# Two layer norms moved into the blocks that use them, x turned in the experts' block, single steps first, idle products on TensorE

## The reference, cut to what matters

```python
for layer in range(2):
    u = x * (1.0 + sc1) + sh1
    mix = _mixer(u, w_in[layer], ...)                 # conv, gated linear attention
    x = _layernorm(ALPHA * x + (1.0 + g1) * mix, ln1_g[layer], ln1_b[layer])
    u = x * (1.0 + sc2) + sh2
    if layer % 2 == 0:
        ff = _dense_swiglu(u, w_gate, w_up, w_down)   # 2816 hidden
    else:
        ff = _moe_swiglu(u, w_router, ...)            # 8 experts, top 2, 2816 hidden
    x = _layernorm(ALPHA * x + (1.0 + g2) * ff, ln2_g[layer], ln2_b[layer])
```

## Time and profile before

| what | value |
|---|---|
| three runs, median (lowest to highest) | 4841.65 us (4836.25 to 4850.41) |
| profiled execution, whole | 4848.16 us |
| its span in the profile | 4846.3 us |
| TensorE products busy | 4079.7 us (84%) |
| VectorE busy | 2875.5 us (59%) |
| ScalarE busy | 1662.4 us (34%) |
| GpSimd busy | 1418.9 us (29%) |
| mean DMA rate | 237 GB/s |

### The profile page before, as it was taken

The page is one execution under the profiler, slowest core; times in us unless marked ns, Lnnn a source line. Parts: engine busy times, 40 slices in busy tenths (PEclk is TensorE's granted clock), DMA queues, the critical chain, the costliest instruction groups (busy, mean ns, idle before and its releaser), DMA issues. The chain is left out here.

```text
span 4846.3 us, 43572 instructions
## 1 busy us (share of the span) xinstructions
PE 4079.7 (84%) x14930; PEld 2725.5 (56%) x14930; DVE 2875.5 (59%) x4171; ACT 1662.4 (34%) x2193; POOL 1418.9 (29%) x1231
## 2 busy tenths in 40 slices
PE   4988997986776766767978998977999999999995
PEld 3864543432322322323756875755878777787774
DVE  4886656565655665652364365454475664747886
ACT  2222402221211212212314323323364554646775
POOL 0430003666666666664413442310000000000000
PEclk7998998998999999999988999988999999999998
DMA  4225086999999999995312263206585765857995
GB/s 151 96 82 199 1 278 251 372 374 362 370 367 367 364 371 366 373 369 213 96 40 70 95 232 124 84 18 247 187 332 189 265 252 194 327 190 296 354 361 199
DMA packets 260053, 1147.99 MB, mean 237 GB/s; under 512 B 28832, under 2 KB 28832, under 8 KB 212512
## 3 DMA queue, kind: packets, MB, share of 16 engines
q0 software_dynamic: 150768, 549.00, 29.7%
q1 hardware_dynamic: 87792, 516.46, 29.5%
q10 hardware_dynamic: 21312, 80.15, 4.5%
HBM read 1131.33 MB, written 14.16 MB: 236 GB/s over the span
## 5 line engine op out<-in xcount | busy, mean ns | idle before, releaser
L1340 PE MATMUL psum<-row,diag 128*128 128x512 f32 x1632 | 802.4, 639 | 297.5 <-DMA row<-in_peer_v,expert 124.3
L1340 PEld LDWEIGHTS psum<-row,diag 128*128 128x128 f32 x1632 | 316.8, 203 | 771.7 <-issue 505.1
L1171 DVE CUSTOM_DVE_ANT_0 row<-row,psum 128x1024 f32<-128x1024 f32 x412 | 497.4, 1219 | 309.7 <-DMA row<-in_peer_u,expert 213.6
L1138 POOL DMA_INDIRECT row<-in_peer_u,expert x412 | 392.7, 953 | 561.9 <-DVE expert L1084 425.8
L2159 PE MATMUL psum<-exp_high,exp_xt 128*128 128x512 f32 x1320 | 527.3, 400 | 28.4 <-DVE exp_low L2275 17.3
L2159 PE MATMUL psum<-exp_high,exp_xlow 128*128 128x512 f32 x1320 | 517.7, 392 | 0.0
L2159 PE MATMUL psum<-exp_low,exp_xt 128*128 128x512 f32 x1320 | 515.7, 391 | 0.0
L1138 POOL DMA_INDIRECT row<-in_peer_v,expert x408 | 385.7, 945 | 255.8 <-issue 121.2
L1252 ACT ACTIVATE diag<-consts_sb,coef 128x128 f32<-128x128 f32 x512 | 175.2, 395 | 591.2 <-PE psum L1340 229.7
L2117 POOL COPY exp_number<-moe_slot_token 128x1 uint32 (+1 forms) x15 | 7.2, 482 | 1211.7 <-PE psum L2138 1155.9
L2159 PEld LDWEIGHTS psum<-exp_high,exp_xt 128*128 128x128 f32 x1320 | 248.9, 189 | 83.3 <-DVE exp_low L2275 17.4
(11 more groups left out here) (464 smaller groups left out, 8007.8 us busy)
## 6 DMA issues: line engine op xcount, KB each, us to landing
exp_wring<-in_moe SPq DMA_DIRECT2D x99, 1024.0 KB, 6.1
h<-in_moe SPq DMA_DIRECT2D x66, 1024.0 KB, 6.0
squares<-in_moe SPq DMA_DIRECT2D x66, 1024.0 KB, 6.5
x<-in_moe SPq DMA_DIRECT2D x66, 1024.0 KB, 6.6
slab_ring<-in_moe SPq DMA_DIRECT2D x66, 1024.0 KB, 5.8
slab_ring<-in_w_in SPq DMA_DIRECT2D x92, 512.0 KB
mix_rows<-in_ada ACTq DMA_DIRECT2D x48, 512.0 KB, 5.2
squares<-in_ada ACTq DMA_DIRECT2D x48, 512.0 KB, 6.4
```

Of the source, the lines that this page charges most:

```text
L1138: pool.indirect_dma_start(out=s.row[row % ROWS], out_offset=None, in_=table, in_offset=bass.IndirectOffsetOnAxis(ap=s.expert[:, g, j:j + 1 ...
L1171: dve.tensor_tensor_reduce(at, at, tokens[g // PH], 1.0, 0.0, ALU.mult, ALU.add, s.act[:, g % 2, j:j + 1]).then_inc(row_used.sem, 1)
L1340: mm = pe.matmul(sums[:, half * T:(half + 1) * T], s.diag[:, (PTOP * g + j) % DIAGS, :], s.row[row % ROWS][:, half * T:(half + 1) * T], st ...
```

## The change

- Two `normalise` blocks go. `norm_act`, `norm_dve` and `norm_pe` do the same norm at the head of `dense_up` and of layer 1's `mix_in`. Gains and shifts of norm and modulation are folded (`fold`), so h and its rounded half are made straight from the scaled x; the map of x itself comes later, one tile at a time, behind evictions. The first two slabs are multiplied together, tile by tile (`fine_pair`), and the low-rank product of `mix_in` follows them.
- `dense_down` keeps a running sum of x and ends with one product for the mean; `second_gains` stands ahead of its last eviction.
- `spin` gives TensorE products of 256 columns whose result nobody reads: 4 ahead of a wait for the sum of x (`residual`, `dense_down`), 4 ahead of the squares and 16 (13 in `route`) behind them, 6 in `run_experts`.
- Turning, copying and writing x move from `route` to the head of `run_experts`; the DMAs are issued by ScalarE instead of SyncE.
- The experts' loop is (single, double); one token block is turned ahead of it instead of two, and VectorE splits slab 0 ahead of that block.

```diff
+    def norm_act(self, act, s, eps, scale, bias):
+        for k in range(KT):
+            act.wait_ge(centred.sem, centred.at(k + 1))
+            act.activation(self.squares[:, k, :], self.x[:, k, :], ACT.Square).then_inc(squared.sem, 1)
+        act.wait_ge(summed.sem, summed.at(1))
+        act.activation(self.stat[:, 0, :], self.side[:, 0, :], ACT.Sqrt, bias=self.eps[eps], scale=1.0 / D).then_inc(rooted.sem, 1)
+        for k in range(KT):
+            act.wait_ge(scaled.sem, scaled.at(k + 1))
+            act.activation(self.h[:, k, :], self.x[:, k, :], ACT.Identity, scale=scale(k), bias=bias(k)).then_inc(normed.sem, 1)
+            act.activation(s.hhigh[:, k, :], self.x[:, k, :], ACT.Identity, scale=scale(k), bias=bias(k)).then_inc(rounded.sem, 1)
+    def norm_dve(self, dve, s, gain, bias, scale, shift):
+        dve.tensor_tensor(s.fold[:, 0, :], gain, scale, ALU.mult).then_inc(folded.sem, 1)
...
+        for k in range(KT):
+            dve.scalar_tensor_tensor(self.x[:, k, :], self.side[:, 1, :], -1.0 / D, self.x[:, k, :], ALU.mult, ALU.add).then_inc(centred.sem, 1)
+        dve.wait_ge(rooted.sem, rooted.at(1))
+        dve.reciprocal(self.stat[:, 1, :], self.stat[:, 0, :]).then_inc(inverted.sem, 1)
...
+        for k in range(KT + 1):
+            if k < KT:
+                dve.tensor_tensor(self.x[:, k, :], self.x[:, k, :], self.stat[:, 1, :], ALU.mult).then_inc(scaled.sem, 1)
+            if k:
+                dve.wait_ge(normed.sem, normed.at(k))
+                dve.wait_ge(rounded.sem, rounded.at(k))
+                dve.tensor_tensor(s.hlow[:, k - 1, :], self.h[:, k - 1, :], s.hhigh[:, k - 1, :].bitcast(F32), ALU.subtract).then_inc(split.sem, 1)
+    def spin(self, pe, n):
+        for _ in range(n):
+            pe.matmul(self.side[:, 3, 0:2 * P], self.const("ones"), self.consts[:, 0:2 * P], start=True, stop=True)
+    def norm_pe(self, pe):
+        self.spin(pe, 4)
+        for k in range(KT):
+            pe.wait_ge(squared.sem, squared.at(k + 1))
+            mm = pe.matmul(self.side[:, 0, :], self.const("ones"), self.squares[:, k, :], start=k == 0, stop=k == KT - 1)
+        mm.then_inc(summed.sem, 1)
+        self.spin(pe, 16)
+    def fine_pair(self, pe, s):
+        pe.wait_ge(split.sem, split.at(2))
+        for k in range(KT):
+            pe.wait_ge(h_split.sem, h_split.at(k + 1))
+            for slot in range(2):
+                for n, (w, x) in enumerate(((s.high, s.hhigh), (s.low, s.hhigh), (s.high, s.hlow))):
+                    mm = pe.matmul(self.bank[:, slot, :], w[:, slot, at], x[:, k, :], ...)
+                if k == KT - 1:
+                    mm.then_inc(self.slab_used, 1)
...
@@ mix_in @@
+                if layer:
+                    self.norm_pe(pe)
+                    self.fine_pair(pe, s)
...
-                self.round_source(act, s, self.h)
+                if layer:
+                    self.norm_act(act, s, LN_EPS, lambda k: s.fold[:, 0, k:k + 1], lambda k: s.fold[:, 1, k:k + 1])
...
+                    if layer and SLOTS < i <= SLOTS + KT:
+                        act.activation(self.x[:, k, :], self.x[:, k, :], ACT.Identity, scale=gain(k), bias=bias(k))
@@ dense_down @@
+                self.spin(pe, 4)
+                pe.wait_ge(x_summed.sem, x_summed.at(KT - 1))
+                pe.matmul(self.side[:, 1, :], self.const("ones"), s.sum[:], start=True, stop=True).then_inc(averaged.sem, 1)
...
+                    if i == KT - 1:
+                        self.second_gains(dve, 1)
...
+                        dve.tensor_tensor(s.sum[:], s.sum[:] if i > 1 else self.x[:, 0, :], self.x[:, i, :], ALU.add).then_inc(x_summed.sem, 1)
@@ route @@
+                self.spin(pe, 4)
...
+                self.spin(pe, 13)
...
-                for f in range(FLIPS, 2 * FLIPS):
-                    copy(f)
@@ run_experts @@
         def double(i):
-            return dict(step=2 * i, doubles=i, width=2, block=3 * i, place=[2 * i, 2 * i + 1], ring=[0, 1], flips=[(3 * i + 2, 2)])
+            return dict(step=2 * i + 1, doubles=i, width=2, block=3 * i + 1, place=[2 * i, 2 * i + 1], ring=[1, 2], flips=[(3 * i + 3, 0)])
         def single(i):
-            return dict(step=2 * i + 1, doubles=i + 1, width=1, block=3 * i + 2, place=[2 * DOUBLES + i], ring=[2],
-                        flips=[(3 * i + 3, 0), (3 * i + 4, 1)])
+            return dict(step=2 * i, doubles=i, width=1, block=3 * i, place=[2 * DOUBLES + i], ring=[0],
+                        flips=[(3 * i + 1, 1), (3 * i + 2, 2)])
...
+                for f in range(FLIPS):
+                    half, t = divmod(f, TT)
+                    for k in range(4):
+                        mm = pe.transpose(self.side[:, 2 + f % 2, k * P:(k + 1) * P], self.x[:, 4 * half + k, t * P:(t + 1) * P], self.const("ident"))
+                    mm.then_inc(x_flipped.sem, 1)
+                pe.wait_ge(x_copied.sem, x_copied.at(FLIPS))
+                self.spin(pe, 6)
+                for half in range(2):
+                    flip(0, half)
...
+                for t in range(TT):
+                    act.wait_ge(x_copied.sem, x_copied.at(TT + t + 1))
+                    act.dma_start(s.kept_x[t * P:(t + 1) * P, :], s.xn[:, t, :]).then_inc(x_kept.sem, 16)
                 for i in range(AHEAD):
                     round_slab(0, i)
...
-                for n in range(2):
-                    for half in range(2):
-                        x_half(n, n, half)
-                for i in range(AHEAD):
+                split_slab(0, 0)
+                for half in range(2):
+                    x_half(0, 0, half)
+                for i in range(1, AHEAD):
                     split_slab(0, i)
```

More of the change, by code:

```diff
@@ L384, in fetch_row, with fine_rest, close_norm @@
+    def fine_rest(self, pe, s):
+        product = self.fine(pe, s, ready=None)
+        for j in range(2, SLOTS):
+            pe.wait_ge(self.taken, self.used + j - SLOTS + 1)
+            product(j, j).then_inc(self.slab_used, 1)
+    def close_norm(self):
+        for name, n in (("centred", KT), ("squared", KT), ("summed", 1), ("rooted", 1), ("inverted", 1), ("scaled", KT), ("normed", KT), ("folded", 3)):
+            self.sig(name).close(n)
     def fetch_row(self, eng, s, rows, columns, n):
@@ L1407, in experts, with mix_in @@
         self.used += n
-    def mix_in(self, s, layer):
+    def mix_in(self, s, layer, gain=None, bias=None, gains=None, biases=None, scale=None, shift=None):
         base = self.used
@@ L1694, in residual, with dense_up @@
         self.used += KT
-    def dense_up(self, s):
+    def dense_up(self, s, gain, bias, gains, biases, scale, shift):
         base = self.used
@@ L1733, in _ @@
                         high(f - 1)
+                    if part and f < KT:
+                        act.activation(self.x[:, f, :], self.x[:, f, :], ACT.Identity, scale=gain(f), bias=bias(f))
                 high(FT - 1)
@@ L2105, in _ @@
                 with sp.Fori(0, DOUBLES) as i:
+                    slabs(single(i), i + DOUBLES)
                     slabs(double(i), i)
-                    slabs(single(i), i + DOUBLES)
                 for j in range(TAILS):
@@ L2126, in _ @@
                 with pool.Fori(0, DOUBLES) as i:
+                    gathers(single(i))
                     gathers(double(i))
-                    gathers(single(i))
                 for j in range(TAILS):
@@ L2255, in _ @@
                 with act.Fori(0, DOUBLES) as i:
+                    step(single(i))
                     step(double(i))
-                    step(single(i))
                 for j in range(TAILS):
```

114 lines of the change are left out of this document (70 added, 44 removed).

## The result

| kernel | runs | median us (lowest to highest) |
|---|---|---|
| changed | 4 | 4790.42 (4784.22 to 4795.94) |
| before, beside it | 4 | 4840.36 |

The ratio is 0.9892, 95% interval 0.9875 to 0.9909. The forecast was 4790 us (4772 to 4815), faster at 0.94.

A forecast was written before the change was run, and what follows sets the result against it. TensorE bounds the stages; at the seams the chain of ScalarE, VectorE and small products does. Gains 15.0 + 11.4 + 12.9 + 12.5 = 51.8 us from 4848.2 give 4796.4, by the median 4790 us; range 4772 to 4815.

The forecast's parts named there:

- the charge of 1.7: Behind the experts' start: 1.0 us lost to a fourth pair of flips in the first tail, 0.7 to the clock.
- First norm: Head of dense_up: 60.3 us falls to 42.8, gain 17.5, less 2.5 for a fallen clock: 15.0 us.
- rival (d): Both norms: VectorE waiting behind GpSimd paces the slab pair, 4 us lost in each; 4798 us, chance 0.05.
- Second norm: Head of mix_in: 68.9 us falls to 54.5, less 2.5 for the clock and 0.5 for VectorE: 11.4 gained.
- Router, sums and logits: Router: idle products cut the sums from 9.37 to 7.1 us (2.3) and the logits from 13.82 to 9.1 (4.7).
- Router, the flips of x: Router's end: with x's flips gone, the next block begins at 3290.0 instead of 3295.9; 5.9 us gained.
- the router's sum: Router: sums 2.3, logits 4.7 and moved flips 5.9 add to 12.9 us gained, bounds 5 to 16.
- Experts' start: From the experts' block to its first product: 31.7 us falls to 17.5, gain 14.2 us.
- The first single step takes about 100 us: Experts' loop: sign of a right forecast, the first single step lasting about 100 us from the first product.
- (b): First expert step runs short of slabs, so the start's gain comes back as waits; 4802 us, chance 0.14.
- (c): Same slab supply shortage in the first expert step but worse, slower than before; 4852 us, chance 0.03.
- Rival (a): Idle products don't hold the clock: 9 less in first norm, 6 in second, 7 in router; 4812 us, chance 0.13.

The follow-up runs named there:

- first pair: The first profiled executions of the kernel before and the changed kernel: 4848.16 and 4784.22 us.
- second pair: Both kernels unchanged, run and profiled again on one other chip: ratios to the kernel before 0.9883 (changed) and 0.9997 (before).
- low_rank_later: Changed kernel with ScalarE rounding slabs 2 and 3 in mix_in ahead of its copy of the low-rank product; ratio to the kernel before 0.9873.
- small_idle: Changed kernel with each idle product of 256 columns replaced by four of 8 columns; ratio to the kernel before 1.0043.
- x_in_router: Changed kernel with turning, copying and writing of x back at the router's end, by SyncE; ratio to the kernel before 0.9901.
- double_first: Changed kernel with the experts' loop (double, single) again and two token blocks turned and split ahead of it; ratio to the kernel before 0.9917.
- no_idle: Changed kernel with no idle products anywhere; ratio to the kernel before 0.9921.
- slabs_in_turn: Changed kernel with the pair's two loops exchanged, slab 1 multiplied after slab 0 instead of interleaved; ratio to the kernel before 0.9903.
- ring_order: Changed kernel with the experts' weight ring taking slab_ring's two buffers ahead of those of h, squares and x; ratio to the kernel before 0.9880.

## Why the prediction was right

The sum, 51.8 us, stands against 52.1 and 49.8 measured in the stretches. That the total agrees within 2 us is partly luck: the router fell short by 3.5, and in the first pair the rest of the second norm's stretch (2.1 more than forecast) and the charge of 1.7 that did not show made up for it. Point by point:

- **First norm**, 15.0: measured 15.0 and 14.7. Each part came: 7.13 for the sums, the gap to slab 2 (32.2 us after the mean product, forecast 31.6), the fallen clock behind it. The centring beside GpSimd cost nothing, and the pair ends 29.2 us after the mean product (forecast 28.7), which disposes of rival (d).
- **Second norm**, 11.4: 11.4 and, in the second pair, 8.9 from the last product of dense_down to the fourth slab. As forecast, nothing of ScalarE's rounding hides in the low-rank product; low_rank_later showed that this was a choice of order that costs 5 to 7 us.
- **Router, sums and logits**, 2.3 and 4.7: 2.3 and 4.3. The estimate that the clock falls part of the way through the logits was right, in every run with idle products of 256 columns. This is where I weighed the Trainium skill (TensorE: Matmul & The Clock Gate, What's actually happening), by which the gate follows how busy TensorE has been. The logits' window at 0.51 with 5.00 of 5.00 us busy, and small_idle's at 0.50 with 6.00 of 6.00, disagree with it in that form.
- **Router, the flips of x**, 5.9: at equal clock 5.7 to 5.8 (x_in_router against double_first, before against no_idle), so this step stands. But the tail of the changed kernel is shorter by 2.8 us only, in both pairs. The step that failed is the router's sum, "2.3 + 4.7 + 5.9": it let the clock of the logits end with the logits. Before, they ran at half clock from their start and the clock was back for the ranking products (0.96 us for eight). In the changed kernel it falls late in the logits and comes back late, so these products and the flips between them run at half clock (1.72 us), VectorE and the copies wait for them, and 3 us of the 4.3 won in the logits are lost. Of the six traces of this router three (the two of the changed kernel and slabs_in_turn) have it so, and in the other three (ring_order, low_rank_later and double_first) the clock was back in time (tail 19.3 to 19.4); what decides between them no run shows. The router gave 9.4, not 12.9.
- **Experts' start**, 14.2: 14.8 and 14.6. The terms on the path came within 0.5 us, counted from the block's start: last copy of x 7.1 (forecast 7.1), DMA issues 8.5 (8.9), rounding 10.5 (10.8), split 12.8 (13.1), two halves 4.1 (4.2). Beside the path two were off: the first gathered tile was there at 11.5 and not 9.9, and slab 5 was issued at 24.9 and not near 20, 20.7 us of which SyncE waited for x's write; neither held up TensorE. double_first shows that it is the order of the steps.
- **The charge of 1.7** behind the start cannot be seen in the pairs (-0.6 and +1.8 over 1472 us, within what executions differ by). "The first single step takes about 100 us" was too low: 104.4 to 106.8 in ten runs, a little over the 102.90 of the later single step in the earlier trace rows, from which it should have been taken. It is not set by x's write, for neither x_in_router nor ring_order shortens it, nor by the loads at 410 GB/s, since TensorE waits for no slab; TensorE is busy 99.55 us in it, with its clock at 0.98, against 95.79 in the next single step. Rivals (b) and (c) needed it to be longer than 110 us. The double step behind it gives most of that back (191.6 us, where the first double took 195.0 before); by the third eviction the single-first order is 2.9 us later in the mean of the traces (double_first, above).
- **Rival (a)**, idle products that do not hold the clock, priced at 22 us. no_idle's ratio puts them all at 14, give or take some 10, so even with no effect at all the time would have been near 4802 (0.9921 of 4840.36). Most of the gain, some 38 us of 52, comes from the orders: the norm beside the slabs, x out of the router, and one token tile instead of two.

## What to carry to other kernels

Before a block of a norm, look whether its chain (squares, root, scaling) can run beside the next block's weight preparation and hand over tile by tile; it gave 26 us in two places here, some 8 of them (2.0 and 6.1, no_idle) by the idle products. When work is moved off the end of a block, list what each engine still has queued ahead of the last result, not only the engine that came last: here a map of 5.7 us on ScalarE took over at once. A set of idle products is worth a few us where a wait stands ahead of real work; count them so that they end just before the data come, because too few give almost nothing (44 that ended 4.5 us early gave 0.3) and too many delay the list (22.6 us).

## What the runs showed of the hardware that was not expected

- In products of 8 columns the granted clock fell from 1.00 to 0.50 although TensorE was busy all the time (logits, 3215 to 3225 us of the changed kernel; in small_idle from 0.82 over 2561 to 2568 to 0.50 behind it), and it came back to 1.00 in full-width products after that (L445 0.63 us at the pair's start in small_idle, 0.39 from 3.4 us on). The phase of it moves: the router from the first logit to the experts' block took 31.4 us in both traces of the changed kernel and 28.1 and 29.7 in ring_order and low_rank_later, whose router is the same.
- The stretch ahead of layer 0's low-rank product, the same instructions in all kernels, took 2270.8 to 2290.6 us in the profiles of the slower chips; on the fast chip they took 2144.5 to 2147.6. The first norm (276.5 to 278.1 us in every trace of the changed norm with idle products of 256 columns) and dense_down's 124 do not differ so, and the medians of the kernel before differ by 133 us (4720.39 against 4853.75), so nearly all of it lies ahead of the second part.
